# A hybrid gMLP and attention block: gaps behind the blocks of high parts in two of four ring slots

## Time and profile before

| | us |
|---|---|
| median of 3 runs | 1588.41 (1588.21 to 1588.43) |
| profiled execution | 1588.61 |
| its span, first to last instruction | 1586.8 |
| TensorE busy | 1577.7 (99%) |
| VectorE busy | 1260.4 (79%) |
| ScalarE busy | 828.1 (52%) |

### The profile page before, as it was taken

The page is one execution under the profiler, slowest core; times in us unless marked ns, Lnnn a source line. Parts: engine busy times, 40 slices in busy tenths (PEclk is TensorE's granted clock), DMA queues, the critical chain, the costliest instruction groups (busy, mean ns, idle before and its releaser), DMA issues.

```text
span 1586.8 us, 24342 instructions
## 1 busy us (share of the span) xinstructions
PE 1577.7 (99%) x8652; PEld 1367.8 (86%) x8652; DVE 1260.4 (79%) x1836; ACT 828.1 (52%) x1124; POOL 1.9 (0%) x12
## 2 busy tenths in 40 slices
PE   9999999999999999999999999999999999999998
PEld 8888888888888888888888888888888888888886
DVE  6556677677797788777787777877778899989999
ACT  6544544456565654444444444444444575766664
POOL 0000000000000000000000000000000000000000
PEclk9999999999999999999999999999999999999999
DMA  9895455556566465556555566655666555555552
GB/s 371 267 232 190 160 185 163 181 160 203 194 241 217 152 210 187 186 185 200 190 190 185 185 197 190 195 185 185 195 189 198 199 208 207 208 198 200 185 212 106
DMA packets 234946, 313.15 MB, mean 197 GB/s; under 512 B 5360, under 2 KB 209808, under 8 KB 234000
## 3 DMA queue, kind: packets, MB, share of 16 engines
q1 hardware_dynamic: 231056, 306.44, 58.5%
q10 hardware_dynamic: 3840, 6.05, 1.5%
HBM read 309.58 MB, written 2.88 MB: 197 GB/s over the span
## 4 chain that ended last, share of the span: by engine, by line
PE 96%; DVE 4%; issue 0%; ACT 0%; DVEq 0%
PE ps L1494 44%; PE ps L1498 23%; PE ps L1585 15%; PE ps L1778 6%; PE ps L1635 3%; PE ps L1598 1%; DVE actT L1189 1%; DVE w_lo L1189 1%; PE ps L1509 1%; PE ps L1514 0%; DVE arena L1177 0%; PE ps L1724 0%; PE ps L1705 0%; PE ps L1657 0%; PE ps L1717 0%
## 5 line engine op out<-in xcount | busy, mean ns | idle before, releaser
L1494 PE MATMUL ps<-actT,w_hi 128*128 128x512 f32 x3072 | 715.4, 390 | 0.0
L454 ACT ACTIVATE w_hi<-raw 128x1024 fp32r<-128x1024 f32 x420 | 433.4, 1056 | 509.0 <-PE ps L1494 256.9
L862 DVE TENSOR_TENSOR w_lo<-raw,w_hi 128x1024 fp32r<-128x1024 f32 x422 | 506.1, 1223 | 236.8 <-ACT w_hi L454 234.5
L1494 PEld LDWEIGHTS ps<-actT,w_hi 128*128 128x128 f32 x3072 | 569.4, 188 | 113.0 <-issue 0.2
L1498 PEld LDWEIGHTS ps<-actT,w_lo 128*128 128x128 f32 x3072 | 378.2, 188 | 9.9 <-issue 1.7
L1498 PE MATMUL ps<-actT,w_lo 128*128 128x256 f32 x3072 | 384.4, 281 | 0.0
L1585 PE MATMUL ps<-w_hi,xs 128*128 128x512 f32 x832 | 226.6, 389 | 0.0
L1585 PEld LDWEIGHTS ps<-w_hi,xs 128*128 128x128 f32 x832 | 156.1, 188 | 32.4
L1585 PE MATMUL ps<-w_lo,xs 128*128 128x512 f32 x416 | 128.1, 389 | 0.0
L1189 DVE TENSOR_TENSOR w_lo<-raw,w_hi 128x1024 fp32r<-128x1024 f32 x96 | 117.3, 1222 | 0.0
L1379 DVE SCALAR_TENSOR_TENSOR arena<-arena,convw 128x256 f32<-128x256 f32 x256 | 106.8, 480 | 0.0
(11 more groups left out here) (181 smaller groups left out, 935.7 us busy)
## 6 DMA issues: line engine op xcount, KB each, us to landing
raw<-in_w_up_dram SPq DMA_DIRECT2D x128, 1024.0 KB, 5.5
raw<-in_w_down_dram SPq DMA_DIRECT2D x64, 1024.0 KB, 5.2
raw<-in_w_in_dram SPq DMA_DIRECT2D x58, 1024.0 KB, 5.2
raw<-in_w_o_dram SPq DMA_DIRECT2D x16, 1024.0 KB, 5.3
raw<-in_w_a_out_dram SPq DMA_DIRECT2D x8, 1024.0 KB, 5.3
raw<-in_w_b_out_dram SPq DMA_DIRECT2D x8, 1024.0 KB, 5.2
arena<-in_x_dram SPq DMA_DIRECT2D x1, 2048.0 KB, 17.1
arena<-in_x_dram ACTq DMA_DIRECT2D x2, 1024.0 KB, 6.1
```

Source lines behind the costliest of these rows:

```text
L454: act.activation(w_hi[:, h % RING, :], raw[:, h // 2, h % 2 * HALF:(h % 2 + 1) * HALF], ACT.Copy)\
L862: dve.tensor_tensor(lo, raw[:, h // 2, h % 2 * HALF:(h % 2 + 1) * HALF], w_hi[:, h % RING, :].bitcast(F32), ALU.subtract).then_inc(lo_read ...
L1494: return pe.matmul(ps[:, bank + c, :], w_hi[:, h % RING, at:at + P], actT[:, k, :, :].rearrange("p a s -> p (a s)"), start=start, stop=stop)
```

## The change

The buffer of `w_hi` gets slots of 1152 instead of 1024 numbers. `w_hi` stays as a view of the first 1024 of each slot, and beside it there is a view by blocks for each slot, `w_hi_blocks`, in which the blocks stand 128 + pad numbers apart, with pads 0, 0, 16 and 4 for slots 0 to 3: 512, 512, 576 and 528 bytes. ScalarE's and VectorE's splits take the block view in feature-major stages (by argument, `padded` and `feature_major`), and `by_hi` reads its stationary block from it. The start of block 0 of a slot, the low parts' places and all other stages' views stay as they are. The high parts for token-major stages and for the first turn of the up-projection are written flat, as before. No instruction is added or removed. The core of the diff (left out: the calls in which an argument is added or renamed):

```diff
-        w_hi = sb("w_hi", [P, RING, HALF], F32R)
+        w_hi_padded = sb("w_hi", [P, RING, HALF + P], F32R)
+        w_hi = w_hi_padded[:, :, 0:HALF]
+        HI_PAD = (0, 0, 16, 4)
+        w_hi_blocks = [w_hi_padded[:, slot, 0:HALF // P * (P + pad)].rearrange("p (b c) -> p b c", c=P + pad)[:, :, 0:P]
+                       for slot, pad in enumerate(HI_PAD)]
...
-            def split(m, h, fresh=False, free=None):
+            def split(m, h, fresh=False, free=None, padded=True):
...
-                act.activation(w_hi[:, h % RING, :], raw[:, h // 2, h % 2 * HALF:(h % 2 + 1) * HALF], ACT.Copy)\
-                   .then_inc(hi_ready, 1)
+                full, hi = raw[:, h // 2, h % 2 * HALF:(h % 2 + 1) * HALF], w_hi[:, h % RING, :]
+                if padded:
+                    full, hi = full.rearrange("p (b c) -> p b c", c=P), w_hi_blocks[h % RING]
+                act.activation(hi, full, ACT.Copy).then_inc(hi_ready, 1)
...
-            def split(m, h, shifted=True):
+            def split(m, h, feature_major=True):
...
-                lo = w_lo_shifted[h % RING] if shifted else w_lo[:, h % RING, :]
-                dve.tensor_tensor(lo, raw[:, h // 2, h % 2 * HALF:(h % 2 + 1) * HALF],
-                                  w_hi[:, h % RING, :].bitcast(F32), ALU.subtract).then_inc(lo_ready, 1)
+                full, hi = raw[:, h // 2, h % 2 * HALF:(h % 2 + 1) * HALF], w_hi[:, h % RING, :].bitcast(F32)
+                lo = w_lo[:, h % RING, :]
+                if feature_major:
+                    full, hi = full.rearrange("p (b c) -> p b c", c=P), w_hi_blocks[h % RING].bitcast(F32)
+                    lo = w_lo_shifted[h % RING].rearrange("p (b c) -> p b c", c=P)
+                dve.tensor_tensor(lo, full, hi, ALU.subtract).then_inc(lo_ready, 1)
...
-                return pe.matmul(ps[:, bank + c, :], w_hi[:, h % RING, at:at + P],
+                return pe.matmul(ps[:, bank + c, :], w_hi_blocks[h % RING][:, at // P, :],
```

More of the change, by code:

```diff
@@ L460, in split_xs @@
                 act.activation(xs[:, h % RING, 0, :], src, ACT.Copy)
-                split(m, h, free=free)
+                split(m, h, free=free, padded=False)
             def copy_out(g, bank, used):
@@ L521, in _ @@
                 split_x(h)
-                split(0, h, fresh=True)
+                split(0, h, fresh=True, padded=False)
             for h, k in ((4, 4), (5, None), (6, 6), (7, None)):
@@ L528, in _ @@
                     split_x(k + 1)
-                split(0, h)
+                split(0, h, padded=False)
             for h, k in ((0, 8), (1, 10), (2, 12), (3, 14), (4, None), (5, None), (6, None), (7, None)):
@@ L533, in _ @@
                     split_x(k + 1)
-                split(1, h)
+                split(1, h, padded=False)
                 if h in (3, 4):
@@ L770, in _ @@
             root(MIX_OUT, 1, 2 * T)
-            split(m, 2)
+            split(m, 2, padded=False)
             split_first_rows(1, 0, 1)
-            split(m, 3)
+            split(m, 3, padded=False)
             split_rows(1, 4, 1)
-            split(m, 4)
-            split(m, 5)
+            split(m, 4, padded=False)
+            split(m, 5, padded=False)
             split_rows(1, 4, 2)
-            split(m, 6)
+            split(m, 6, padded=False)
             act.wait_ge(x1_done, T * (D // XC - 1) + 2)
@@ L781, in _ @@
             split_rows(1, 4, 3)
-            split(m, 7)
+            split(m, 7, padded=False)
             act.wait_ge(x1_done, T * (D // XC) + 1)
@@ L868, in split_xs @@
                 dve.tensor_tensor(xs[:, h % RING, 1, :], src, xs[:, h % RING, 0, :].bitcast(F32), ALU.subtract)
-                split(m, h, shifted=False)
+                split(m, h, feature_major=False)
             def add_out(g, bank, dst):
@@ L936, in _ @@
                     split_x(0)
-                    split(0, 0, shifted=False)
+                    split(0, 0, feature_major=False)
             split_x(1)
-            split(0, 1, shifted=False)
+            split(0, 1, feature_major=False)
             for h in (2, 3):
                 split_x(h)
-                split(0, h, shifted=False)
+                split(0, h, feature_major=False)
             for h, k in ((4, 4), (5, None), (6, 6), (7, None)):
@@ L951, in _ @@
                     split_x(k + 1)
-                split(1, h, shifted=False)
+                split(1, h, feature_major=False)
                 if h == 4:
@@ L1337, in _ @@
             split_rows(1, KD + 2, 1)
-            split(m, 2, shifted=False)
-            split(m, 3, shifted=False)
+            split(m, 2, feature_major=False)
+            split(m, 3, feature_major=False)
             residual(2, 0)
@@ L1342, in _ @@
             split_rows(1, KD + 2, 2)
-            split(m, 4, shifted=False)
+            split(m, 4, feature_major=False)
             residual(3, 0)
             residual(3, 1)
-            split(m, 5, shifted=False)
+            split(m, 5, feature_major=False)
             split_rows(1, KD + 2, 3)
-            split(m, 6, shifted=False)
-            split(m, 7, shifted=False)
+            split(m, 6, feature_major=False)
+            split(m, 7, feature_major=False)
             for t in range(T):
```

## The result

The changed kernel takes **1598.11 us** (median of 4 runs, 1597.88 to 1598.27), the kernel before 1588.42 (1588.21 to 1588.55): ratio 1.0061, 95% interval 1.0049 to 1.0074. It is 9.7 us slower. The forecast was 1586.7 with a range up to 1592.0; the time lies in what the prediction called rival C.

What follows compares the result with a forecast made beforehand. The prediction took the distance of TensorE's matmul starts as the bound. From the profiled 1588.61 us, -2.7 and +1.0 gave 1586.9, or 1586.7 us against the timed median, range 1583.3 to 1592.0.

Steps and rivals of the forecast that it cites:

- rival C: High products on TensorE: gaps break their even pace, +7.0 us, 1595.4 us, or 1600.2 at the higher price; chance 0.22.
- (a): Stationary reads of high parts in slots 2 and 3: 1344 moved blocks gain 2 ns each, -2.7 us.
- (b): Way back from shifted to aligned blocks, once more for each of 96 groups: 10 ns each, +1.0 us.
- (c): ScalarE's split writes eight runs of 512 bytes instead of one of 4096: covered, counted 0.
- (d): VectorE's subtraction takes the padded form as input: no charge for the form, counted 0.
- (e): Stages left alone keep the flat view; no instruction, wait or transfer added: counted 0.
- Rival B: High products: nothing moves, the 13.3 ns beside the columns are a fixed price; 1588.4 us, chance 0.22.
- Rival D: High products: full gain, 2.5 ns off all 1536 and no second return, -4.8 us, 1583.6 us; chance 0.20.

Runs made afterwards that it cites:

- experiment 6: Changed kernel with all gaps at 0 and the low parts of the feature-major stages without their shifts: 1594.74 us, ratio 1.0041 to the kernel before.
- Experiment 4: Changed kernel with the gaps of 16 and 4 numbers in slots 0 and 1 instead of 2 and 3: 1595.98 us, ratio 1.0049 to the kernel before.
- Experiment 2: Changed kernel with gaps of 512 bytes in slots 2 and 3, every block at a multiple of 512 bytes: 1588.38 us, ratio 1.0000 to the kernel before.
- experiment 1: Changed kernel with all four gaps at 0, wide slots and block views kept: 1588.23 us, ratio 1.0001 to the kernel before.
- experiment 3: Changed kernel with constant shifts of 64 and 16 bytes in slots 2 and 3 instead of gaps: 1598.24 us, ratio 1.0064 to the kernel before.
- experiment 11: Kernel before with all four low shifts at 8 bytes, nothing else changed: 1583.59 us, ratio 0.9970 to the kernel before.
- experiment 10: Scan within the up-projection: low parts 8 bytes off, high parts in wide slots without gaps at eight offsets in turn; one run, only its trace used.
- experiment 12: Gaps of 256 bytes in slots 2 and 3, every other block 256 bytes off, against experiment 2: 1588.44 us, ratio 1.0001 to the kernel before.
- experiment 8: Kernel before with the low parts' shifts varied within the up-projection, equal in all slots, beside today's mixed set; one run, only its trace used.

## Why the prediction was wrong

- **What bounds the kernel** was read rightly: only the distance of TensorE's starts could change the time, and the whole loss is one row of TensorE.
- **(a), the stationary reads,** is the step that failed. It took -2 ns for a moved block from the low parts' rows "because it is the only place in which the placing of the stationary block itself is the variable". The low parts' gain is true (experiment 6), but it does not carry over to 512 moving columns. The padded slots cost 94 - 12 = 82 cycles more, 68 ns for each of 96 groups: **+6.6 us in place of -2.7**. For a moved block, 14 of the 16, that is +4.9 ns, between the 3.3 and the 6 ns which the prediction had from the earlier trace rows as its upper bounds.
- **(b), the way back,** was the right mechanism at the right place, once a group where slot 0 follows slot 3, and too small: 46 cycles, 38 ns, in place of 10: **+3.7 us in place of +1.0**. The row of 27 ns that it had as the upper end was nearer, and itself short: there the way back begins from low products. Experiment 4 takes this term out: the kernel is 2.1 us faster. That is less than 3.7 in the main because, with the gaps in slots 0 and 1, the two slow products behind the low parts (12 cycles or 10 ns a group, 1.0 us) come on top again, which in the changed kernel are within the 94. Some 0.6 us are left over; the sums count 96 whole groups, of which 11 are broken, and that explains a part of it, as it does where the main sum of 10.3 stands against 9.7 measured.
- **(c) and (d), the splits,** were right at nothing: 1056 and 1222 ns, and no piece of ScalarE or VectorE between the products in the chain shown. Experiment 2 confirms it with the same eight runs at no cost. **(e)** was right too: 32 low products at 3.78, L1594 (the old L1585) has 226.6 us as before, and experiment 1 costs nothing.
- **Rival C** was the case that came true: its row, its place and its sign. Its centre was 1595.4 from 3.3 ns a block and 27 ns a return; with 4.9 and 38 the same sum is 10.3, 1598.7 by its own reckoning, and the measured time is 1598.1. So its mechanism was right; its centre was 2.7 us low, because both prices were. It lost in my weighing because the unsettled rows came behind a stall or a change of width and not behind a shifted block. But they held the comparison that mattered: low products away from their settled 120 ns are faster (118.1), high products away from their settled 226.7 are slower (230). The sign of the effect was in the trace for each width apart, and I let the row with the right cause and the wrong width outweigh the row with the right width.
- **Rival B** was argued with a rule of the Trainium skill, SBUF — State Buffer, section "A bandwidth-pool intuition that's wrong (but worth ruling out)", by which weights have a second, independent read port. That section speaks of ports and not of places; the step from the one to the other was the prediction's, and the runs contradict it: places alone cost 10.0 us in experiment 3 and gain 4.8 in experiment 11. **Rival D** needed high products under 226.7 ns on average; no offset tried gave that.
- My range ended at 1592.0 and cut C's centre off, at a chance of 0.22 for it.

Shown is where the time goes, that the places of the blocks cause it, that neither splits, gaps nor slot distance do, and that the place of the moving operand plays a part too. Not shown is what inside TensorE or its reads makes one place settle at 226.7 ns and another at 233.3, or why 256 and 496 bytes are harmless and 504 isn't. Nor do these runs tell whether it is the reading of the stationary block, of the moving columns or the two together that is slower; the recorded loads of the feature-major stages have means of 188 ns, and 191 for the unshifted low parts of experiment 6.

## What to carry to other kernels

Where TensorE is busy all the time, the start distance of its matmuls is a quantity of its own: read it from the chain or the starts, for each shape apart, and look for products that are slower only behind a change. An offset in on-chip memory that gains a little for one width of moving columns can lose for another; a scan over offsets that varies them by pieces of one loop costs one run and is read from the trace. Keep the blocks that have settled where they are, and count for every unsettled stretch also the way back of the ones behind it.

## What the runs showed that I had not expected

- An fp32r product of 512 columns keeps 226.7 ns to the next at offsets of 0, 256 and 496 bytes (experiments 10 and 12), 13.3 ns above its columns at 2.4 GHz, and about 233.3 at rest at 16 bytes (experiment 3, slot 3). One of 256 columns goes from 120.0 (no offset) to 115 to 116.7 (8 bytes).
- TensorE needs up to nine products to settle (nine behind low parts that are 16 bytes off, 56 cycles in all, experiment 8), and the sequence of distances on the way (280 283 269 277 283 274 279 277 cycles) is nearly the same behind padded blocks, behind a shifted slot and, cut short, behind low products: 280 283 274 279 277 in experiment 6. One group is an exception. In experiment 10 the first whole group at 496 bytes, behind slots at 504, kept distances of 270 to 276 through all its 32 products (7.31 us) before the next came to 7.28. So 496 bytes keep the settled pace but have not been seen to bring it back within one run.
- A shift of the moving operand by 64 bytes, with shifted stationary low parts, takes the low products to 3.71 us for 32 and within slot 3, whose low parts lie 128 bytes off, to 136 cycles, 113.3 ns, at rest: the fastest resting pace of any product with 256 moving columns in these runs.
